# Projecting a sample group's queries into the latent space: up-projection as the moving operand, queries stationary in four column groups

## The reference

```
qa     = einsum('bthd,chd->bthc', q_nope * k_norm[:64], w_uk)      # 8 samples, 16 heads, 64 -> 256
s_past = latent_scores(qa, q_rope, past)                            # 1024 cached rows a sample
s_new  = latent_scores(qa, q_rope, rows)                            # the new row itself
p      = softmax([s_past, s_new]);  ctx = p @ latents;  o = ctx @ w_uv
```

## Time and profile before

| | us |
|---|---|
| median of 3 runs | 1502.58 (1500.77 to 1503.23) |
| profiled execution | 1508.13 |
| its span, which the rows count in | 1506.4 |
| PE busy | 1458.2 (97%) |
| DVE busy | 741.2 (49%) |
| ACT busy | 606.4 (40%) |
| POOL busy | 161.9 (11%) |

### The profile page before, as it was taken

How to read it: one execution, slowest core, us unless ns; L and a number is a source line. 1 busy time by engine, 2 the same in 40 slices (tenths; PEclk the granted TensorE clock), 3 DMA queues, 4 the chain that set the end, 5 groups by cost and what they waited for, 6 DMA issues and landing times.

```text
span 1506.4 us, 28877 instructions
## 1 busy us (share of the span) xinstructions
PE 1458.2 (97%) x11672; PEld 1364.5 (91%) x11672; DVE 741.2 (49%) x1244; ACT 606.4 (40%) x949; POOL 161.9 (11%) x194
## 2 busy tenths in 40 slices
PE   7999988889999999999999999999999999999999
PEld 6999987777999999999999867655899999999999
DVE  6887545657964444443233336466444444443222
ACT  5444533445334434332222454467434434432111
POOL 1000022220810000000000001442020000000000
PEclk9999989999999999999999999799999999999999
DMA  5222200004353232333332321465322322233332
GB/s 216 84 84 84 85 0 30 28 29 148 108 200 98 84 97 88 93 90 110 92 91 87 100 85 57 120 190 168 113 85 88 94 87 94 84 97 91 88 90 81
DMA packets 48575, 144.64 MB, mean 96 GB/s; under 512 B 6912, under 2 KB 16224, under 8 KB 47344
## 3 DMA queue, kind: packets, MB, share of 16 engines
q1 hardware_dynamic: 42048, 118.57, 25.2%
q0 software_dynamic: 6160, 20.79, 4.5%
q10 hardware_dynamic: 288, 4.19, 0.7%
HBM read 134.73 MB, written 7.76 MB: 95 GB/s over the span
## 4 chain that ended last, share of the span: by engine, by line
PE 86%; DVE 8%; issue 3%; ACT 2%; DVEq 0%; DMA 0%; ACTq 0%; POOLq 0%
PE PS L561 84%; DVE arena L1847 2%; PE PS L1101 1%; ACT arena L1643 1%; DVE arena L2010 1%; DVE mx L2286 1%; PE PS L817 0%; DVE arena L1837 0%; DVE arena L1842 0%; ACT wsplit L1283 0%; DVE wsplit L1749 0%; DVE arena L2062 0%; DMA gains<-in_gains 0%; DVE arena L1845 0%; ACT arena L1462 0%
## 5 line engine op out<-in xcount | busy, mean ns | idle before, releaser
L561 PE MATMUL PS<-xnh,wsplit 128*128 128x260 f32 x3904 | 639.0, 285 | 12.6 <-DVE wsplit L1749 12.6
L561 PEld LDWEIGHTS PS<-xnh,wsplit 128*128 128x128 f32 x3904 | 541.7, 190 | 15.2 <-DVE wsplit L1749 13.3
L561 PE MATMUL PS<-xnl,wsplit 128*128 128x260 f32 x1952 | 394.8, 284 | 0.0
L1283 ACT ACTIVATE wsplit<-wring 128x1024 fp32r<-128x1024 f32 x176 | 183.0, 1040 | 438.8 <-PE PS L561 434.8
L1749 DVE TENSOR_TENSOR wsplit<-wring,wsplit 128x1024 fp32r<-128x1024 f32 x176 | 210.8, 1198 | 207.0 <-ACT wsplit L1283 207.0
L561 PEld LDWEIGHTS PS<-xnl,wsplit 128*128 128x128 f32 x1952 | 302.4, 190 | 0.0
L561 PE MATMUL PS<-hidh,wsplit 128*128 128x260 f32 x1408 | 226.6, 283 | 0.0
L561 PEld LDWEIGHTS PS<-hidh,wsplit 128*128 128x128 f32 x1408 | 192.9, 188 | 0.0
L561 PE MATMUL PS<-arena 128*128 128x128 f32 (+9 forms) x944 | 162.5, 335 | 15.4 <-DVE arena L2010 10.5
L561 PEld LDWEIGHTS PS<-arena 128*128 128x128 f32 (+2 forms) x944 | 120.3, 192 | 52.8 <-issue 34.9
L561 PE MATMUL PS<-hidl,wsplit 128*128 128x260 f32 x704 | 141.2, 282 | 0.0
(11 more groups left out here) (416 smaller groups left out, 1681.3 us busy)
## 6 DMA issues: line engine op xcount, KB each, us to landing
wring<-in_w_gu SPq DMA_DIRECT2D x88, 512.0 KB, 3.6
wring<-in_w_dn SPq DMA_DIRECT2D x32, 512.0 KB, 3.5
wring<-in_w_proj SPq DMA_DIRECT2D x28, 512.0 KB, 3.6
wring<-in_w_dn SPq DMA_DIRECT2D x16, 384.0 KB, 3.1
wring<-in_w_outa SPq DMA_DIRECT2D x8, 512.0 KB, 4.4
wring<-in_w_inc SPq DMA_DIRECT2D x8, 512.0 KB, 3.5
wring<-in_w_uq SPq DMA_DIRECT2D x8, 512.0 KB, 4.7
wring<-in_w_outc SPq DMA_DIRECT2D x8, 512.0 KB, 4.2
```

The costliest lines, as they stand in the source:

```text
L561: return pe.matmul(out, lhsT, rhs, start=start, stop=stop)
L1283: act.activation(dst[:, 0:w], wring[slot(stage, u)][:, 0:w], ACT.Copy).then_inc(s('w_hi'), 1)
```

## The change

The two operands change places. Now the queries of two heads, `qkn[:, m, :]`, are stationary, 32 columns wide (two heads by 8 samples, and 16 columns of zeros), and the up-projection of the two heads moves, 256 columns. Four such products stand side by side in four column groups of the array and write four strips of 32 rows of bank 7; there are two sets of four, one for each half of the bank. The result has the latent index along the row, so DVE copies the whole bank to `qrows` in SBUF and PE turns it with four 128x128 transposes (`turn_queries`), again into bank 7. The order on PE is now: the eight products in one piece, `score_part(1, 2)`, `score_part(1, 3)`, the four transposes, `turn_probs(0)`. DVE's copy stands in the middle of `sample_columns`, after `j == 1`, behind a wait for the eight products, and raises `gk_ready` to 2; the end of `sample_columns` therefore raises it to 3. ACT takes `qa` out of bank 7 with four copies of 128x64 in place of two of 128x128. Later waits on `sample_mm` and `gk_ready` count one higher.

```diff
-        qkn = nc.alloc_sbuf_tensor_at("qkn", [128, 8, 2, NS], F32, offset=outlo1_at + 4 * 640)
+        qkn = nc.alloc_sbuf_tensor_at("qkn", [128, 8, 32], F32, offset=outlo1_at + 4 * 512)
+        qrows = sq[:, :, :].rearrange("p a t -> p (a t)")[:, 0:512]
...
             pool.wait_ge(s('s_mm'), 3 * 12)
-            pool.wait_ge(s('gk_ready'), 2)
+            pool.wait_ge(s('gk_ready'), 3)
             pool.dma_start(wuv, A['w_uv']).then_inc(g_loaded, 16)
...
                 pe.wait_ge(s('gk_ready'), 1)
-                for m in range(MH // 2):
-                    if m in (2, 4):
-                        score_part(1, m // 2 + 1)
-                    for k in range(2):
-                        e = (k * 8 + m) * 2 * NS
-                        ins = mm(PS[:, 7, e:e + 2 * NS], wukt[:, m, k * 128:(k + 1) * 128], qkn[:, m].rearrange("p e b -> p (e b)"))
+                for half in range(2):
+                    for g in range(4):
+                        m = 4 * half + g
+                        ins = mm(PS[32 * g:32 * g + 32, 7, half * 256:(half + 1) * 256], qkn[:, m, :], wukt[:, m, :])
+                ins.then_inc(s('sample_mm'), 1)
+                score_part(1, 2)
+                score_part(1, 3)
+
+            def turn_queries():
+
+                pe.wait_ge(s('gk_ready'), 2)
+                for e in range(4):
+                    ins = pe.transpose(PS[:, 7, e * 128:(e + 1) * 128], qrows[:, e * 128:(e + 1) * 128], ident)
                 ins.then_inc(s('sample_mm'), 1)
...
                     sample_queries()
+                    turn_queries()
...
                 if i == 1:
-                    pe.wait_ge(s('gk_ready'), 2)
+                    pe.wait_ge(s('gk_ready'), 3)
                     sample_new()
...
                 if i == 0:
-                    act.wait_ge(s('sample_mm'), 2)
-                    for k in range(2):
-                        ins = act.activation(qa[:, k, :, 0:16].rearrange("p b h -> p h b"),
-                                             PS[:, 7, k * 128:(k + 1) * 128].rearrange("p (h b) -> p h b", b=NS), ACT.Copy)
+                    act.wait_ge(s('sample_mm'), 3)
+                    for half in range(2):
+                        for k in range(2):
+                            to = qa[:, k, :, 8 * half:8 * half + 8].rearrange("p b (g e) -> p g e b", e=2)
+                            at_ = half * 256 + k * 128
+                            turned = PS[:, 7, at_:at_ + 128].rearrange("p (g e b) -> p g e b", g=4, b=NS)[:, :, 0:2, :]
+                            ins = act.activation(to, turned, ACT.Copy)
                     ins.then_inc(s('so_ready'), 1)
...
-            st(dve.memset(qkn[:, :, :, :], 0.0))
+            st(dve.memset(qkn[:, :, :], 0.0))
...
-                st(dve.tensor_copy(qkn[64 * e:64 * e + 64, :, e, :], qhat[0:64, e::2, T:TOK]))
+                st(dve.tensor_copy(qkn[64 * e:64 * e + 64, :, NS * e:NS * e + NS], qhat[0:64, e::2, T:TOK]))
...
                     st(dve.tensor_copy(invn[32 * j:32 * j + 16, :], invr[:, T + j:TOK:4]))
+                    if j == 1:
+                        dve.wait_ge(s('sample_mm'), 2)
+                        st(dve.tensor_copy(qrows, PS[:, 7, :]), s('gk_ready'))
```

More of the change, by code:

```diff
@@ L1686, in _ @@
             for rnd in range(ROUNDS):
-                act.wait_ge(s('sample_mm'), 4 + ROUNDS)
+                act.wait_ge(s('sample_mm'), 5 + ROUNDS)
                 for k in range(2):
@@ L1693, in _ @@
                 out_high(m)
-            act.wait_ge(s('sample_mm'), 7)
+            act.wait_ge(s('sample_mm'), 8)
             for e in range(2):
@@ L2305, in new_scores @@
             def new_scores():
-                dve.wait_ge(s('sample_mm'), 3)
+                dve.wait_ge(s('sample_mm'), 4)
                 st(tt(smx[:, :, 4], PS[:, 7, 0:ROUNDS], invn[:, :], ALU.mult), s('snew_ready'))
@@ L2373, in _ @@
                     pair_scaled((i - 3) // 2)
-            dve.wait_ge(s('sample_mm'), 4)
+            dve.wait_ge(s('sample_mm'), 5)
             dve.wait_ge(s('spt_mm'), NUNIT // 2)
```

## The result

| | before | changed |
|---|---|---|
| median, 20 runs each | 1502.59 us (1500.61 to 1506.19) | 1500.38 us (1495.56 to 1502.20) |
| ratio of the two | | 0.9978, 95% interval 0.9968 to 0.9988 |
| span of the profiled execution | 1506.4 us | 1495.1 us |

The account below looks back on a forecast made before the run. PE bounds the kernel, paying for loading stationary tiles and perhaps the half clock behind. 2.44 + 1.11 - 0.05 + 0.66 + 0.9 = 5.06 us off 1502.58 gives 1497.5 us; own range 1496.5 to 1498.5 (52%), wide range 1493.2 to 1500.3.

Parts of the forecast that it names:

- Products, copy, start of `turn_probs(0)`, start of `sample_new`: Sample queries: products 1.00 us, DVE copy 0.65 us, `turn_probs(0)` starting at 950.45, `sample_new` at 951.70.
- it and not the transposes decides: Before `turn_probs(0)`: `exps(0)`, ending at 950.31, sets PE's start at 950.45; the transposes are done at 950.30.
- 4.04 us: Cost of the removed 16-column query products on PE, taken as 5.17 - 1.13 us from the profile before.
- I expect the clock to hold until about its end and fall there: Full clock until about `sample_new`'s end, then half for `key_unit(0)` and `scores(2)`, back for `turn_probs(1)`, 0.9 us gained.
- The runs lie 5.6 us under the profiled time: 1502.58 - 5.06: Last step: the whole 5.06 us gain taken off the runs' 1502.58 us, giving 1497.5 us.
- 1.11 + 0.66 + 0.9: Gains in us forecast from full clock in place of half: `turn_probs(0)` 1.11, `sample_new` 0.66, `turn_probs(1)` 0.9.
- the second rival: Clock falls at 951.9 as before, fourteen transposes weighing as narrow work; gain only 3.5 us, 1499.1 us; 18%.
- That the clock does not fall: Rival: dense work around `sample_new` keeps 2.4 GHz, so `key_unit(0)` and `scores(2)` gain too; 8.6 us, 1494.0 us; 13%.
- That half clock lasts long: Rival: clock falls at 955 and stays half for 17 us, through `key_unit(1)` and `values(0)`; gain 0.6 us, 1502.0; 9%.
- given back later: Rival: from 1017 on, where ACT shares the chain, gain is lost, leaving 0 to 2.5 us, 1501 us; 5%.
- slower: Rival: products neither overlap nor have full clock, taking 7.2 us, and DVE work queues behind them; 1505.8 us; 3%.
- That VectorE would hold PE: Queries pass through DVE: copy stalls PE 0 to 0.12 us; `sample_new` 2.6 us later if products take 7.2 us.

Follow-up runs that it names:

- both: Changed kernel with `sample_new`'s products ordered by column group and VectorE's twelve small copies moved ahead of the loop; ratio 0.9952 against the kernel before, median 1496.73 us.
- order_only: Kernel before with its sixteen 16-column products in one piece and `score_part(1, 2)`, `score_part(1, 3)` behind them; ratio 0.9987, median 1500.92 us.
- before_late1: Kernel before with one clearing of 1040 columns on GpSimd ahead of its first load, starting about a microsecond later; 1502.87 us, one execution.
- after_again: Changed kernel run once more, unchanged; ratio 0.9972 against the kernel before, median 1500.08 us.
- pad_dense: Changed kernel with 24 more products of the same form, computing nothing, right after the eight that count; ratio 0.9981 against the kernel before, median 1499.44 us.
- one_group: Changed kernel with all eight products written to the same column group; ratio 0.9974 against the kernel before, median 1499.98 us.
- after_shift: Changed kernel with `score_part(0, 0)` computed two more times ahead of itself; ratio 0.9990 against the kernel before, median 1503.39 us.
- new_grouped: Changed kernel with `sample_new`'s 24 one-column products ordered so that four neighbours fall into four column groups; ratio 0.9977 against the kernel before, median 1501.00 us.

## Why the prediction was nearly right

**Products, copy, start of `turn_probs(0)`, start of `sample_new`: right**, each within 0.1 us of the forecast, the four groups' overlap with them. The cause given for the start of `turn_probs(0)`, "it and not the transposes decides", is not borne out: `exps(0)` ends at 947.86, PE starts at 947.91 without idle time, and in `both` the chain runs through the transposes. The 1.10 us for ten transposes is not in the earlier trace rows, but the changed kernel has 1.09. The one wrong number is the cost of the old products. 4.04 us came from a profile whose clock fell at 951.9, so its last products were already at half clock; order_only has them at 3.57. The direct gain up to `turn_probs(0)` at full clock is 3.57 + 1.13 - 2.66 = 2.04 us, not 2.44; before_late1, at full clock up to there, has 4.65 us for products and scores together, which gives 1.99.

**"I expect the clock to hold until about its end and fall there": right** in the first four profiles of the changed kernel. `turn_probs(0)` and `turn_probs(1)` were at full clock (1.26 to 1.31 and 1.26 us). `sample_new` took 2.99 us where 3.3 was taken from the ratio of two records. What came back sooner than forecast is `scores(2)`: 2.67 instead of 4.6. In the profile the place therefore gained 7.4 us where the sum said 5.06, and the profiled execution came out at 1496.79 us where 1503.1 was forecast.

**The step that was mis-sized is the last: "The runs lie 5.6 us under the profiled time: 1502.58 - 5.06".** Three of its terms, 1.11 + 0.66 + 0.9 = 2.67 us, are differences between half and full clock in one profiled execution, and they were subtracted from a median of executions most of which, by their mean clock, have less half clock to lose. The 5.6 us were themselves the sign: they are not the price of profiling but the distance between an execution at a mean clock of 0.985 and the usual ones at 0.987 to 0.989. Measured were 3.3 us by the ratio instead of 5.06. With the direct 2.04 that leaves about 1.3 for the clock instead of 2.67 (3.3 - 2.04; worked out, not measured by itself). The split is uncertain: after_again's ratio gives 4.2 us in all, and at equal time at half clock the two kernels differ by only 0.8 to 1.0 us, which would leave more to the clock. The ratio puts the time at 1499.3 us, inside the range; the median of 1500.38 lies 0.08 above its upper end. The forecast's own range, 1496.5 to 1498.5, was missed. By the number alone the second rival (1499.1) was nearest, and its mechanism did not occur; that the wide range holds the ratio's time is luck in part, since it was that wide for rivals that did not come true.

**The rivals.** That the clock does not fall happened in the profiles of pad_dense, one_group and `both`, not in the changed kernel's. That it falls as early as before did not happen in any of them: PE did the transposes from 947.44 on and all of `sample_new` before the fall at 952.6. The rule that this rival rests on (the Trainium skill, TensorE: Matmul & The Clock Gate, Part 4: a transpose does not count as busy the way a product does) is neither shown nor refuted by that; no run here takes the transposes by themselves. That half clock lasts long, given 9% at 17 us, happened in part in after_shift, 10.2 us, and the timed executions at 0.987, 7 of 32, fit it. It deserved more. Nothing was given back later in the changed kernel's profile: from `key_unit(1)` to the end it took 535.9 us for 537.3. Nothing was slower. That VectorE would hold PE was priced, but only for products that take too long; it holds PE as the change is written, by about 0.1 us (`sample_new` begins 4.03 us after the products, 3.95 in `both`, where VectorE's copies are out of the way), and shows its price once `sample_new` is short (new_grouped against both).

**What made the gain.** Shown: with the direct saving undone (pad_dense, one_group) there is still a gain of 2.9 to 3.9 us, so less time at half clock can carry a gain of this size alone; the old operands in another order (order_only) gain 2.0. Not shown: that the clock is the larger part in the changed kernel itself, because the padding also changes when and after what work `sample_new` comes. Argued only: that the share of wide work around the moment decides. Why the kernel before stayed at half clock for 17 us in one place and 10 in another was not settled, since the length also moved with the moment.

## What to carry to other kernels

Narrow products on TensorE can be paid twice, in their own time and in the half clock that may follow; here a wider form paid even where it was no shorter (pad_dense, 2.9 us). Before subtracting a saving from the median, compare the mean granted clock of the profiled execution with that of the timed runs, and take terms of clock only in the proportion in which those runs show it. After an engine has been relieved, look at once at who ends its next wait: the shorter `sample_new` brought `key_unit(0)` only 0.4 us nearer until VectorE's small copies had gone. And look at half clock in places that the change does not touch: in the 14 profiles here it differs by up to 6.8 us at half clock, which by half that time (an estimate) is as much as the change is worth.

## What the hardware showed unexpectedly

The same kernel spent 10.2 or 16.8 us of the same 30 us at half clock, and the changed one 3.6 or 10.2, with nothing but the work or the start in front of it moved. The timed executions lie in groups by their mean clock, with means from 1495.6 to 1502.1 us, or 1500.8 to 1508.1 before; how much of that is this place is open. Half clock does not cost the same everywhere: `sample_new` with its single columns took 3.96 us at half and 2.99 at full clock, 1.3 times, the 256-column products of `key_unit` 1.94 and 1.07, 1.8 times. Ordering the 24 products of `sample_new` by column group brought 2.99 us down to 0.85, where 1.6 had been expected.
